# A trunk of two layers on one core: the first two up blocks of an MLP quarter as one pair with seven-product sets

## What is computed

```python
def rmsnorm(x, g):
    y = xf * lax.rsqrt(jnp.mean(xf * xf, axis=-1, keepdims=True) + EPS)
    return (y * g.astype(jnp.float32)).astype(x.dtype)

def sq_relu_mlp(hn, w1, w2):
    return jnp.square(jax.nn.relu(hn @ w1)) @ w2

        h = h + sq_relu_mlp(rmsnorm(h, ln_mlp[i]), mlp_w1[i], mlp_w2[i])
```

## Time and profile before

| | us |
|---|---|
| three runs | 2524.52, 2524.63 (median), 2525.1 |
| profiled execution, its own time | 2525.19 |
| its span | 2523.5 |
| PE busy | 2515.6 |
| DVE busy | 1827.6 |
| ACT busy | 1488.9 |
| granted TensorE clock | 0.999 of 2.4 GHz, every slice of the page at 9 |

### The profile page before, as it was taken

One profiled execution on the slowest core, in us unless ns is written; L12 is line 12 of the kernel. 1 busy time (PEld: TensorE's weight loads), 2 busy tenths in 40 slices (PEclk: granted clock), 3 DMA queues, 4 the chain that ended last, 5 costly groups with the idle time before them and its releaser, 6 DMA issues.

```text
span 2523.5 us, 29875 instructions
## 1 busy us (share of the span) xinstructions
PE 2515.6 (100%) x11496; PEld 2086.8 (83%) x11496; DVE 1827.6 (72%) x2046; ACT 1488.9 (59%) x1814; POOL 103.2 (4%) x208
## 2 busy tenths in 40 slices
PE   9999999999999999999999999999999999999999
PEld 8888888888888888888888888888888888888887
DVE  6778787878768668668577667767686785775765
ACT  6755556655565465564556667655654645546653
POOL 2010000000000000000001002100000000000000
PEclk9999999999999999999999999999999999999999
DMA  8877888887686776766767764458867667677873
GB/s 279 239 238 242 236 246 239 232 230 219 196 212 192 228 197 205 217 187 229 213 204 227 217 185 142 141 159 211 206 204 221 186 225 214 183 226 201 230 219 131
DMA packets 344815, 530.29 MB, mean 210 GB/s; under 512 B 131664, under 2 KB 137032, under 8 KB 344672
## 3 DMA queue, kind: packets, MB, share of 16 engines
q1 hardware_dynamic: 340496, 518.16, 70.1%
q0 software_dynamic: 2656, 8.58, 1.4%
q10 hardware_dynamic: 1520, 1.64, 0.2%
HBM read 486.38 MB, written 2.16 MB: 194 GB/s over the span
## 4 chain that ended last, share of the span: by engine, by line
PE 100%; DMA 0%; DVE 0%; ACT 0%; ACTq 0%; issue 0%
PE acc_a L2199 9%; PE acc_a L2201 9%; PE acc_a L2200 9%; PE acc_b L2199 9%; PE acc_b L2201 9%; PE acc_b L2200 9%; PE mid L2199 3%; PE mid L2200 3%; PE mid L2201 3%; PE tp L2200 2%; PE tp L2201 2%; PE tp L2199 2%; PE acc_a L2214 2%; PE acc_b L2214 2%; PE mid L2216 2%; PE mid L2215 2%
## 5 line engine op out<-in xcount | busy, mean ns | idle before, releaser
L1400 DVE TENSOR_TENSOR w<-raw,w 128x1024 fp32r<-128x1024 f32 (+1 forms) x816 | 986.2, 1218 | 472.1 <-ACT w L742 467.6
L742 ACT ACTIVATE w<-raw 128x1024 fp32r<-128x1024 f32 (+1 forms) x844 | 883.2, 1053 | 675.4 <-PE acc_b L2201 216.0
L2199 PE MATMUL acc_a<-w,xa 128*128 128x512 f32 x760 | 298.4, 393 | 0.0
L2201 PE MATMUL acc_a<-w,xa 128*128 128x512 f32 x760 | 296.1, 390 | 0.0
L2200 PE MATMUL acc_a<-w,xa 128*128 128x512 f32 x760 | 295.7, 389 | 0.0
L2199 PE MATMUL acc_b<-w,xa 128*128 128x512 f32 (+1 forms) x736 | 285.6, 388 | 0.0
L2201 PE MATMUL acc_b<-w,xa 128*128 128x512 f32 (+1 forms) x736 | 283.1, 385 | 0.0
L2200 PE MATMUL acc_b<-w,xa 128*128 128x512 f32 (+1 forms) x736 | 282.9, 384 | 0.0
L2201 PEld LDWEIGHTS acc_a<-w,xa 128*128 128x128 f32 x760 | 142.7, 188 | 30.0
L2200 PEld LDWEIGHTS acc_a<-w,xa 128*128 128x128 f32 x760 | 142.8, 188 | 28.7
L2199 PEld LDWEIGHTS acc_a<-w,xa 128*128 128x128 f32 x760 | 142.8, 188 | 28.7
(11 more groups left out here) (417 smaller groups left out, 4674.5 us busy)
## 6 DMA issues: line engine op xcount, KB each, us to landing
raw<-in_mlp_w SPq DMA_DIRECT2D x512, 512.0 KB, 4.5
raw<-in_ssm_in_w SPq DMA_DIRECT2D x161, 512.0 KB, 5.9
raw<-in_ssm_out_w SPq DMA_DIRECT2D x64, 512.0 KB, 5.3
raw<-in_ple_gate_w SPq DMA_DIRECT2D x64, 512.0 KB, 4.1
raw<-in_mla_out_w SPq DMA_DIRECT2D x32, 512.0 KB, 3.9
scratch<-cumulative POOLq DMA_DIRECT2D x16, 512.0 KB, 7.0
rows<-in_ssm_conv_w SPq DMA_DIRECT2D x32, 256.0 KB, 6.4
raw<-in_ple_proj_w SPq DMA_DIRECT2D x8, 512.0 KB, 4.5
```

The lines of the kernel that those rows point to most:

```text
L742: act.activation(w_hi[:, g % SPL, :, 0:cols], raw[:, g % RAW, :, 0:cols], ACT.Copy)\
L1400: dve.tensor_tensor(w_lo[:, g % SPL, :, 0:cols], raw[:, g % RAW, :, 0:cols], w_hi[:, g % SPL, :, 0:cols].bitcast(F32), ALU.subtract).then_ ...
L2199: pe.matmul(dst, xh, wh, start=first and k == 0, stop=False)
L2201: mm = pe.matmul(dst, xl, wh, start=False, stop=last and k == 1)
```

## The change

- Up blocks 0 and 1 of quarters 1, 2 and 3 become one *up pair* of 20 ticks, `pair_unit` over `xa` with two seven-product sets. Up blocks 2 and 3 stay units of 8. The opening 16 chunks of quarter 0 stay.
- The sets of the up pair are over the last four tiles of the input (`UP_ORDER` puts groups 6 and 7 third and sixth). Their activation sums are made once per layer, in the opening 16 chunks, and kept (`xs` grows from 2 to 4 sets).
- The results of the shared products gather in SBUF (`up_shared`, behind ticks 18 and 19), the pair's own banks are added behind tick 3 of up block 2 (`up_all`, twice, signal cf), and ACT takes the half-words from there (`unzip_sums`).
- In every pair the weight sums move: `first_differences` 4 ticks ahead of the set, `second_sums` 3, with a wait that the slots written to are free.
- `turn_block` of quarters q > 0: behind chunks 6 and 7 of up block 2, chunk 6 of up block 3, tick 11 of the first down pair.
- First down pair: ACT's join goes from tick 8 to 9, DVE's square from 8 to 10, `up_lo(3)` from 10 to 12. Bank pairs no longer alternate with q.

The constant and SP's list:

```diff
+UP_ORDER = 0, 1, 6, 2, 3, 7, 4, 5
...
                     if q:
-                        unit(up, c512(q * D + 512))
-                        unit(up, c512(q * D + 2 * 512), jobs={3: [turn_block]})
-                        unit(up, c512(q * D + 3 * 512), jobs={3: [turn_block]})
+                        unit(up, c512(q * D + 2 * 512), jobs={6: [turn_block], 7: [turn_block]})
+                        unit(up, c512(q * D + 3 * 512), jobs={6: [turn_block]})
...
-                    rows_of_pair(down, 0, q * KT, {3: [turn_block], 11: [turn_block]})
+                    rows_of_pair(down, 0, q * KT, {3: [] if q else [turn_block], 11: [turn_block]})
                     if q < 3:
                         rows_of_pair(down, 2, q * KT)
-                        unit(up, c512(q * D + D))
+                        rows_of_pair(up, 4 * q + 4, order=UP_ORDER)
```

ACT's:

```diff
+            def unzip_sums(c):
+                def job(before):
+                    n = w.tick("wd")
+                    words = words_of_two[n % 2]
+                    act.wait_ge(S["cf"], w.tick("cf") + 1)
+                    act.wait_ge(S["jn"], n - 1)
+                    for t in range(NT):
+                        src = shared_sums[t][c].bitcast(U16).rearrange("p (n s) -> p s n", s=2)
+                        last = act.activation(words[:, t], src, ACT.Copy)
+                    last.then_inc(S["wd"], 1)
...
-                        unit({3: [unzip(0, ub)], 7: [join_up]})
-                        unit({1: [up_hi(0)], 3: [unzip(1, ub)], 7: [join_up]})
+                        pair_unit({18: [first_shared(two[0])]})
+                        unit({3: [unzip_sums(0)], 4: [unzip_sums(1)], 6: [join_up], 7: [up_hi(0)]})
...
-                    unit({0: [] if q else [join_up], 1: [up_hi(1)], 3: [unzip(2, ub)], 4: [sums_hi(0)], 7: [join_up]})
-                    pair_unit({1: [up_hi(2)], 3: [unzip(3, ub)], 4: [sums_hi(1)], 8: [join_up], 9: [up_hi(3)], 18: [first_shared(ub[0])]})
+                    unit({1 if q else 0: [join_up], 2: [up_hi(1)], 3: [unzip(2, two)], 5: [sums_hi(0)], 7: [join_up]})
+                    pair_unit({1: [up_hi(2)], 3: [unzip(3, two)], 4: [sums_hi(1)], 9: [join_up], 11: [up_hi(3)],
+                               18: [first_shared(two[0])]})
```

DVE's, with `first_differences`' wait, `after`, `up_shared` and the table of `mlp`:

```diff
+                    dve.wait_ge(S["lo"], w.at("G", g - RAW + 4))
...
-                        if before + tick == g - 2:
+                        if before + tick == g - 4:
                             first_differences(g)
-                        elif before + tick == g - 1:
+                        elif before + tick == g - 3:
                             second_sums(g)
...
+                    def start(before):
+                        on("p1")
+                        own(dve.tensor_tensor(right, p6[:, :], first, ALU.add))
+                        own(dve.tensor_tensor(below, p7[:, :], right, ALU.add))
+                    def end(before):
+                        dve.tensor_tensor(right, p5[:, :], right, ALU.add)
+                        signal(dve.tensor_tensor(last, p5[:, :], below, ALU.add), "sv")
...
-                        unit({7: [square]})
-                        unit({1: [up_lo(0)], 7: [square]})
-                        unit({1: [up_lo(1)], 2: [x_sums_of_seven(0, q_t[:, 0:2])], 5: [sums_lo(0)], 7: [square]})
+                        pair_unit({3: [down(2, b[0]), down(3, b[1])], 18: [shared[0]], 19: [shared[1]]})
+                        unit({3: [up_all(0, a[0]), up_all(1, a[1])], 6: [square], 7: [up_lo(0)]})
+                        unit({1: [square], 3: [up_lo(1)], 4: [x_sums_of_seven(0, q_t[:, 0:2])], 6: [sums_lo(0)],
+                              7: [square]})
...
-                    pair_unit({1: [up_lo(2), x_sums_of_seven(1, q_t[:, 2:4])], 5: [sums_lo(1)], 8: [square],
-                               10: [up_lo(3)], 18: [shared[0]], 19: [shared[1]]})
+                    pair_unit({1: [up_lo(2), x_sums_of_seven(1, q_t[:, 2:4])], 5: [sums_lo(1)], 10: [square],
+                               12: [up_lo(3)], 18: [shared[0]], 19: [shared[1]]})
```

PE's:

```diff
                 for q in range(4):
-                    for j in range(1 if q else 2, 4):
-                        up(j, mine)
+                    if q:
+                        pair_unit(xa, 2, one, two, "cf", made, order=UP_ORDER)
+                        w.skip("wd", 2)
+                    for j in range(2, 4):
+                        up(j, two)
...
-                        up(0, other)
```

More of the change, by code:

```diff
@@ L286, in trunk_kernel @@
             "sv",
+            "cf",
             "dv", "po",
@@ L403, in unit, with rows_of_pair @@
                         job()
-            def rows_of_pair(weight, n, r0=0, jobs=None):
+            def rows_of_pair(weight, n, r0=0, jobs=None, order=range(KT // 2)):
                 v = row_tiles(weight)
@@ L1495, in job @@
                     a = [[first[:, k, t * P:t * P + P] for k in range(2)] for t in range(NT)]
-                    s1, s2, s3, s4 = (r_sb[:, 1, n * P:n * P + P] for n in range(4))
+                    s1, s2, s3, s4 = (r_sb[:, 1, k * P:k * P + P] for k in range(4))
+                    dve.wait_ge(S["xs"], w.now("xs"))
                     dve.tensor_tensor(s3, a[0][0], a[1][0], ALU.subtract)
@@ L1845, in down, with up_shared, up_all, job @@
                     return job
-                one, two = tmp[:, 0:2, :].rearrange("p a n -> p (a n)"), tmp[:, 2:4, :].rearrange("p a n -> p (a n)")
+                one, two = shared_rows
+                def up_shared(banks):
+                    (_, p6), (p5, p7) = (acc[b] for b in banks)
+                    (first, right), (below, last) = shared_sums
+                    def start(before):
[5 more added lines that the diff above has]
+                        signal(dve.tensor_tensor(last, p5[:, :], below, ALU.add), "sv")
+                    return start, end
+                def up_all(c, pair):
+                    def job(before):
+                        dve.wait_ge(S["used"], before)
+                        dve.wait_ge(S["sv"], w.now("sv"))
+                        for t in range(NT):
+                            v = shared_sums[t][c]
+                            done = dve.tensor_tensor(v, acc[pair][t][:, :], v, ALU.add)
+                        done.then_inc(S["cf"], 1)
+                    return job
                 def add_shared(n, banks):
@@ L1891, in mlp @@
                 qq = pp[1], pp[0]
-                unit({2: [down(0, other[0])], 3: [down(1, other[1])], 6: [join, gained(0)]})
+                unit({2: [down(0, a[0])], 3: [down(1, a[1])], 6: [join, gained(0)]})
                 unit({0: [lo(tiles(xa, 0))], 1: [lo((pt[0][:, :, :], pt[1][:, :, :]), tp[:, 0:2, :])],
@@ L2216, in three, with pair_unit @@
                 return pe.matmul(dst, x_lo, wh, start=False, stop=last)
-            def pair_unit(x, banks, shared, event, ready, need=None):
+            def pair_unit(x, sums, banks, shared, event, ready, need=None, order=range(KT // 2)):
                 hold(banks, event)
@@ L2230, in pair_unit @@
                         pe.wait_ge(S["act"], need[m // 2])
+                    tile = 2 * order[m]
                     if m in SEVENS:
@@ L2233, in pair_unit @@
                         first, last = n == 0, n == len(SEVENS) - 1
-                        s1, s2, s3, s4 = ([xs_both[:, n, part, k * P:k * P + P] for part in range(2)] for k in range(4))
+                        s1, s2, s3, s4 = ([xs_both[:, sums + n, part, k * P:k * P + P] for part in range(2)] for k in range(4))
                         pe.wait_ge(S["xs"], ready + n)
@@ L2239, in pair_unit @@
                         pe.wait_ge(S["lo"], g + 1)
-                        three(p1[:, :], *x_part(2 * m, 0), g, 0, first, last)
+                        three(p1[:, :], *x_part(tile, 0), g, 0, first, last)
                         three(p6[:, :], *s2, g, 1, first, last).then_inc(S["used"], 1)
```

70 lines of the change are left out of this document (38 added, 32 removed).

## The result

The changed kernel takes **2537.68 us** (median of 4 runs, 2536.48 to 2540.43) against 2524.60 (4 runs, 2524.52 to 2525.10) of the kernel before on the same chip: a ratio of 1.0053, 95% interval 1.0036 to 1.0070. The prediction had 2521.5 in a range of 2512.5 to 2530. It does less work on PE and takes 13 us more; the range missed it. The profiled execution took 2537.66, with a span of 2535.9.

What follows compares the result with a forecast made beforehand. PE, busy for all of the span, was taken to bound the kernel. From the profiled 2525.2, less 6.9 and 4.6, plus 8.4 for load waits, came 2522.1, or 2521.5 us on the median's scale; range 2512.5 to 2530.

Steps and rivals of the forecast that it cites:

- 36 matmuls fewer, 6.9 us: New up-pair sets: 21 matmuls for 24, 0.57 us each, two sets, three quarters, two layers, saving 6.9 us.
- join and square, 4.6 us: First down pair: moving ACT's join and DVE's square later gives back 0.57 us in each of eight quarters, 4.6 us.
- The 216 and 131 ns: Skill page's matmul paces for 512 columns, by which 36 fewer matmuls would save 7.8 or 4.7 us.
- Up pair, up block 2 and the opening sums at nothing: Added DVE work in these places was claimed to be covered by DVE's lead over PE and cost nothing.
- The chain up to the third transposes: Blocks 2 and 3, q > 0: SP's turns and loads counted from PE's start of up block 2, third turn at 27.0.
- in a row they follow at 1.26 ... so D5 lands at about 41.7: Seven loads behind the third turn land 1.26 us apart; first down pair's tick 5 load at 41.7, first difference waits 1.7.
- my 1.3 to 1.5: First down pair: second difference, behind tick 8, waits 2.6 us for tick 13's load; PE gap 1.3 to 1.5 us.
- The upper bound of 2.7 us a quarter: Chain of blocks 2 and 3: if the second transposes hold SP 4.5 us, V0 1.3 later, 2.7 us a quarter.
- Rival 2: First transposes of block 2 take 4.6 us, gaps at V0, D0, D1, D2, some 5.2 us a quarter: 2544; chance 0.14.
- the 358 GB/s: Skill page's HBM-side bound: 512 KB take 1.46 not 1.26 us, D5 1.2 later, forecast 2529 as an estimate.

Runs made afterwards that it cites:

- The version without gaps: Changed kernel with the first set's sums of every pair back at two and one ticks ahead, second set's at four and three: 2513.36 us.
- experiment 4: Kernel before with only ACT's join and up_hi(3), and DVE's square and up_lo(3), moved later in the first down pair: 2523.13 us.
- experiment 5: Kernel before with the same join and square moves, plus the weight sums of every set four and three ticks ahead: 2520.82 us.
- experiment 9: Changed kernel with the third pair of transposes behind chunk 7 of up block 3 instead of chunk 6: 2528.56 us.
- experiment 2: Changed kernel with only the third pair of transposes moved, from chunk 6 of up block 3 to tick 3 of the first down pair: 2515.28 us.

## Why the prediction was wrong, step by step

- **36 matmuls fewer, 6.9 us; join and square, 4.6 us: right as a sum.** The version without gaps takes 2513.4 for the 2513.1 of 2524.6 - 11.5. The pace of the new sets, 4.86 us, was right, and the rows kept to it (4.86 us by 21 are 0.231 each). The 216 and 131 ns of the Trainium skill, "TensorE: Matmul & The Clock Gate", Back-to-back issue gap, don't agree with these rows. The second term was put down to the join's move alone, which pays 1.9 (experiment 4; 2.1 by the traces); the rest needs the early sums (experiment 5).
- **Up pair, up block 2 and the opening sums at nothing: right.** No gap there in the quarters 1 to 3; quarter 0 of layer 0 keeps one of 0.13 us at tick 9.
- **The chain up to the third transposes: right.** Counted from PE's start of U0 (890.16):

| step | predicted | measured |
|---|---|---|
| first turn starts | 5.9 | 896.01: 5.9 |
| U7's load lands | 12.8 | 898.64 + 4.5: 13.0 |
| V0's load goes out, lands | 12.8, 17 | 903.12, + 4.0: 13.0, 17.0 |
| third turn starts | 27.0 | 917.06: 26.9 |
| V7's load goes out, lands | 29.7, 34.0 | 920.60, + 4.5: 30.4, 34.9 |
| D0's low half ends | 40.0 | 930.95: 40.8 |
| **D5's load lands** | **41.7** | 924.09 + 10.2: **44.1** |
| D2's low half ends | 48.9 | 940.26 + 1.2: 51.3 |
| D13's load lands | 61.1 | 948.98 + 5.6: 64.4 |

- **The step that failed: "in a row they follow at 1.26 ... so D5 lands at about 41.7".** The row of seven loads behind the third turn landed at 1.25, 1.9, 2.2, 1.3, 1.3 and 1.3 us, 9.2 for the six spacings where I had 7.6, and the transposes held SP for 3.5 and not 2.6. The trace of before held such a spacing too: behind the turn at 766.22 the loads issued at 770.74 and 771.36 landed 4.1 and 5.6 us later, 2.1 apart. In the six quarters the six spacings are 8.4 to 10.1 us, 9.0 in the mean; the hold is 3.5 once and 2.6 five times. From D5 on the working holds: 7.2 us to D2's low half predicted (48.9 - 41.7), 7.2 measured. The price goes by D5's landing against PE's start of D0, with the margin already used up:

| D5 lands, from PE's start of D0 | gaps at D0 to D2 |
|---|---|
| change, layer 0: +0.6, +0.2, -0.6 | 2.6, 2.2, 1.4 |
| change, layer 1: -1.2, -1.0, -0.7 | 0.8, 1.0, 1.3 |
| experiment 9, layer 0: -1.3, -1.6, -1.3 | 0.7, 0.4, 0.7 |
| prediction: -1.8 | 0.1 |
| experiment 9, layer 1: -2.2, -1.9, -2.3 | 0, 0.1, 0 |
| experiment 2: -6.2, -5.8, -5.4 | 0 |

Experiment 9 happens to put D5 near where I had it, and there both groups come out near the predicted sizes in most quarters (0.1 and 1.3 to 1.5 predicted; 0.4 to 0.7 and 1.5 to 1.8 measured in layer 0).
- **The second error is that of a chain followed with one value only.** 2.4 us late at D5 were 2.4 us at D2's low half, and then 1.3 to 4.3 us a quarter at D8 to D10 for my 1.3 to 1.5 (1.3 to 2.7 without the clock), since D13's load passes SP behind a turn that itself stands behind D11's. The upper bound of 2.7 us a quarter came from another place (the second turn's hold), with the row of seven loads at its one value of 1.26; 4.0 was measured in the mean. Between experiment 9 and the change D5 is 1.9 us later in quarter 1 and the gaps are 4.3 us longer (6.6 for 2.3), 1.6 of it clock; in quarter 2, 1.8 later and 1.6 longer (3.8 for 2.2). The range had to carry such a slip to both ends of the chain.
- **A term that was not there: the clock.** The chain prices waits alone. Two of the waits were followed by a stretch at 1.2 GHz, 3.2 us together. Of the 15.6 us between forecast and profiled execution (2522.1 and 2537.7) the waits make 12.3 (20.7 for 8.4) and the clock 3.2.
- **Rival 2, the cascade, had the size and not the place.** Its decision point, V0's load landing later than 19.4, was never reached (17.0), and no gap opened at V0. The cascade came one block later.
- The Trainium skill's page "DMA: Bandwidth & Descriptors", Where 436 GB/s comes from, has the 358 GB/s of which I had made 1.46 us a load, as an estimate, where I took 1.26. The mean of the row, 9.0/6 = 1.50, is near it, and I waved it off on two landings. But an even pace is not what the rows show: single spacings are 1.25 and 3.1. With 1.46 throughout the forecast would have been 2529, still 9 us short, since it leaves out what a late D5 does at D8 to D10.

## What to carry to other kernels

Before a consumer is moved ahead, place it against the landing of its input in every stage it runs in, and follow the queue that issues that load; one tick of earliness more was worth nothing here and cost 23 us (2514.4 against 2537.7). A wait that a lead absorbs isn't free: it delays the buffers' release, the queue behind it, and a second wait twenty microseconds on, so price such a chain at both ends of each uncertain term. A long wait can cost more than its length, if the clock falls behind it. And the interval of two landings in one place is no pace for a row of seven loads in another.

## What of the hardware was not expected

- A row of seven 512 KB loads behind a pair of transposes lands unevenly: the first after 4.1 to 4.5 us, the last three 1.25 to 1.29 us apart in all six quarters of the change, the second to fourth 1.25 to 3.1. The row behind the second turn, from the same queue, has 1.28 to 1.37 throughout in layer 0, and one of 2.3 to 2.7 in each quarter of layer 1. What makes the difference (the first rows of another matrix, or something else) wasn't tried and stays open.
- A pair of transposes behind a fresh load holds the issuing queue until that load has landed, wherever it was put: 899.26 + 3.81 = 903.07 against U7's landing at 903.1; 918.90 + 5.12 = 924.02 against D3's at 918.34 + 5.9 = 924.2. With nothing fresh the first and third turns of the change held it 2.6 us in 11 of 12 cases and 3.5 in one (the third turn of quarter 1 of layer 0, which takes 3.6 in experiment 9 too); why is open.
- In three of the twelve quarters (change and experiment 9) the loss behind D8 was 4.0 to 4.7 us for 0.8 to 1.9 in the others. In these three PE stood idle for 2.3, 2.5 and 3.0 us ahead of D9, and within 2 us of its return the granted clock was 0.50 (1.2 GHz) for some 3.4 us, which took 1.6 us each. Behind every other wait of these two traces PE had stood idle for 1.9 us or less, and the clock stayed at 2.4 GHz. Why D13's load was so late in the two of them that lie in layer 1 wasn't settled.
